# A two-layer hybrid trunk on one core: one weight block kept in dead tables, returned rows read last, modulation weights in longer rows, two modulation tiles moved ahead of a wait

## The reference, cut to what matters

```
for layer in range(DEPTH):
    mod = silu(c) @ ada_w[layer] + ada_b[layer]
    sh_m, sc_m, g_m, sh_f, sc_f, g_f = jnp.split(mod, 6, axis=-1)
    h = _modulate(_rmsnorm(x, norm_mix_g[layer]), sh_m, sc_m)
    m = _attn_lru_mixer(h, ...) if layer % 2 == 0 else _s5_mixer(h, ...)
    x = x + g_m[:, None, :] * m
    h = _modulate(_rmsnorm(x, norm_ffn_g[layer]), sh_f, sc_f)
    x = x + g_f[:, None, :] * _hier_moe(h, ...)      # 16 experts, each frame uses 2
return _rmsnorm(x, final_g)
...
he = jax.nn.silu(t @ w1[e]) * (t @ w3[e]);  out = out + gates[:, e:e + 1] * (he @ w2[e])
```

## Time and profile before

| | us |
|---|---|
| median of 3 runs | 868.66 (868.35 to 869.08) |
| the profiled execution | 869.96 |
| its span | 868.2 |
| PE busy | 796.0 (92%) |
| first matmul on expert weights, layer 0 | 194.6 |
| end of the experts of layer 0 | 427 |
| S5 mixer and GLU of layer 1, end of the last GLU matmul | 548 |
| first gather of the experts of layer 1 | 574 |
| last scatter matmul | 855 |

### The profile page before, as it was taken

The page is one execution under the profiler, slowest core; times in us unless marked ns, Lnnn a source line. Parts: engine busy times, 40 slices in busy tenths (PEclk is TensorE's granted clock), DMA queues, the critical chain, the costliest instruction groups (busy, mean ns, idle before and its releaser), DMA issues.

```text
span 868.2 us, 12685 instructions
## 1 busy us (share of the span) xinstructions
PE 796.0 (92%) x5150; PEld 446.4 (51%) x5151; DVE 345.2 (40%) x701; ACT 194.3 (22%) x325; POOL 183.1 (21%) x288
## 2 busy tenths in 40 slices
PE   2799989999999999999879999779999999989694
PEld 0367643576465465565456544334444756536341
DVE  1436996363041141131389895342000313215124
ACT  2402440251131231221441110421001203101112
POOL 2408779217700000000113300050011112101000
PEclk9899989899999999999999999889999999999897
DMA  9999999957999999999981179923788799999991
GB/s 319 346 354 386 352 358 352 330 209 328 422 421 422 421 421 422 422 422 415 396 325 55 44 280 346 373 85 110 303 316 307 276 421 417 420 420 419 419 413 78
DMA packets 72262, 289.65 MB, mean 334 GB/s; under 512 B 9302, under 2 KB 10614, under 8 KB 47384
## 3 DMA queue, kind: packets, MB, share of 16 engines
q1 hardware_dynamic: 66784, 279.98, 82.4%
q0 software_dynamic: 4736, 7.35, 2.5%
q10 hardware_dynamic: 696, 1.68, 0.5%
HBM read 281.64 MB, written 13.63 MB: 340 GB/s over the span
## 4 chain that ended last, share of the span: by engine, by line
PE 76%; DMA 9%; DVE 9%; ACT 2%; issue 2%; SPq 1%; POOL 1%; DVEq 0%; ACTq 0%; POOLq 0%
PE PS L1939 20%; PE PS L1960 13%; PE PS L1968 7%; PE PS L1942 6%; DMA ring<-in_moe_w 6%; PE PS L2315 6%; PE PS L1992 4%; PE PS L1897 4%; PE PS L1659 3%; DMA work<-in_ada_w 2%; PE PS L1689 2%; PE PS L1763 2%; PE PS L1780 2%; SPq L400 1%; PE PS L2300 1%
## 5 line engine op out<-in xcount | busy, mean ns | idle before, releaser
L1960 PE MATMUL PS<-ring,work 128*64 128x512 f32 (+1 forms) x512 | 129.2, 595 | 2.4 <-DMA ring<-in_moe_w 2.4
L1939 PE MATMUL PS<-ring,hT 128*64 128x256 f32 x896 | 109.3, 387 | 9.8 <-DMA ring<-in_moe_w 9.6
L1939 PE MATMUL PS<-ring,yg 128*64 128x256 f32 x896 | 106.3, 379 | 0.0
L1462 DVE TENSOR_TENSOR work<-work,PS 128x512 f32<-128x512 f32 x32 | 22.0, 687 | 204.0 <-PE PS L1939 154.7
L1939 PEld LDWEIGHTS PS<-ring,hT 128*64 128x64 f32 x896 | 63.0, 138 | 51.2 <-DMA ring<-in_moe_w 12.6
L1960 PEld LDWEIGHTS PS<-ring,work 128*64 128x64 f32 (+1 forms) x512 | 42.9, 143 | 75.5 <-issue 69.5
L1939 PEld LDWEIGHTS PS<-ring,yg 128*64 128x64 f32 x896 | 65.0, 137 | 32.1 <-issue 0.4
L1968 PE MATMUL PS<-work,xhat 128*128 128x256 f32 (+1 forms) x256 | 65.7, 415 | 4.5 <-issue 4.5
L697 POOL DMA_INDIRECT y_rows<-yg,row_no x24 | 23.3, 973 | 187.0 <-DVE yg L1470 154.4
L1968 PEld LDWEIGHTS PS<-work,xhat 128*128 128x128 f32 x256 | 48.7, 193 | 23.9 <-issue 17.9
L937 ACT ACTIVATE work<-PS 128x512 f32<-128x512 f32 x32 | 19.1, 597 | 181.2 <-PE PS L1939 119.9
(11 more groups left out here) (415 smaller groups left out, 1043.8 us busy)
## 6 DMA issues: line engine op xcount, KB each, us to landing
ring<-in_moe_w SPq DMA_DIRECT2D x96, 2048.0 KB, 15.8
ring<-in_ada_w SPq DMA_DIRECT2D x20, 2048.0 KB, 16.2
work<-in_ada_w SPq DMA_DIRECT2D x4, 2048.0 KB, 14.0
ring<-in_s_glu_w SPq DMA_DIRECT2D x4, 2048.0 KB, 13.8
ring<-in_ab_w_in SPq DMA_DIRECT2D x3, 2048.0 KB, 24.3
ring<-in_ab_w_out SPq DMA_DIRECT2D x2, 2048.0 KB, 13.1
ring<-rot_tables SPq DMA_DIRECT2D x2, 2048.0 KB, 17.9
rot_tables<-grow POOLq DMA_DIRECT2D x8, 256.0 KB, 5.6
```

The costliest lines, as they stand in the source:

```text
L1462: v.tensor_tensor(pairs_out(he[:, e % 2, :]), pairs_out(he[:, e % 2, :]), pairs(bank[e % 2 * 2 + 1 if direct else 1]), ALU.mult).then_inc( ...
L1939: last = mm(dst[64 * u:64 * u + 64, 0:256], hg[k][:, e * P:e * P + 64], w[:, k, 256 * u:256 * u + 256], start=k == 0, stop=k == KD - 1)
L1960: last = mm(dst, left[:, at:at + (64 if narrow else P)], w[:, c4, h * HALF:(h + 1) * HALF], start=c4 == 0, stop=c4 == KF - 1)
```

## The change

1. `ada_cut`: tiles 0 to 3 are cut the other way. Each still has 2 MB, but holds two of the eight input blocks for all four output units, in rows of 8 KB. The later tiles go in pairs: four input blocks for two units, in rows of 4 KB. `ada` issues the same eight matmuls of 512 columns a tile; `fold` works in 1024 columns, four instructions a tile.
2. In layer 1 the block w2 3 of the last group is not sent last through `ring`. SP sends it into `kept`, where G1 and G0 were, before the loop over the groups, behind a wait for the last S5 output (`y5_ps`) and the first gather of the layer (`gathered`). PE's `down(3)` reads it there.
3. The four reads of `y_rows` are sent after the remaining blocks. `back` moves up by 4096 columns. `add_back(0)` stands in front of `y_out(2)`, `add_back(1)` in front of `y_out(3)`.
4. `ada(22, 24)` leaves `ffn(1)` and stands in front of the wait for `x_new` 3 (the last new rows of the mixer), behind a wait for `x_part` 5; `ffn(1)` opens with one filler matmul (`keep_busy(6, 1)`), as `ffn(0)` does.

```diff
-        back = w3(T0, 2, NB, D)
+        KEPT = PER_GROUP - 1
+        kept = w3(T0, KF, D)
+        back = w3(T0 + SLOT, 2, NB, D)
...
+        def ada_cut(u):
+            n = ADA_FIRST if u < ADA_FIRST else 2
+            first = u - u % n
+            return first, u % n * (KD // n), KD // n, n
...
-                c0 = u % A_UNITS * HALF
-                sp_.dma_start(ada_unit(u), ada_v[u // A_UNITS, :, :, c0:c0 + HALF]).then_inc(
+                first, k0, n_k, n_c = ada_cut(u)
+                c0 = first % A_UNITS * HALF
+                sp_.dma_start(ada_unit(u), ada_v[u // A_UNITS, :, k0:k0 + n_k, c0:c0 + n_c * HALF]).then_inc(
...
+                if L == 1:
+                    sp_.wait_ge(S("y5_ps"), KD)
+                    sp_.wait_ge(S("gathered"), KD * NG + 1)
+                    sp_.dma_start(kept.rearrange("p (u c) n -> p u (c n)", u=2),
+                                  moe_src(L, "w2", (NG - 1) * EPG + ORDER[KEPT][1])).then_inc(S("cn_in"), 16)
                 with sp_.Fori(0, NG - 1) as i:
...
+                for j in range(SLOTS, KEPT if L == 1 else PER_GROUP):
+                    free_slot(n0 + (NG - 1) * PER_GROUP + j)
+                    send_expert(L, j, NG - 1)
                 if L == 1:
                     sp_.wait_ge(S("spread_out"), 64 + 32 * EPG * DIRECT)
...
-                for j in range(SLOTS, PER_GROUP):
-                    free_slot(n0 + (NG - 1) * PER_GROUP + j)
-                    send_expert(L, j, NG - 1)
...
                     y_out(0)
+                    gated(2)
+                    y_out(1)
+                    gated(3)
                     if L == 1:
                         add_back(0)
-                    gated(2)
-                    y_out(1)
+                    y_out(2)
                     if L == 1:
                         add_back(1)
-                    gated(3)
-                    y_out(2)
                     y_out(3)
...
-                if L == 0:
-                    keep_busy(6, 1)
-                else:
-                    ada(ADA_LAST, ADA_ALL)
+                keep_busy(6, 1)
...
+                        if L == 1 and j == KEPT:
+                            pe.wait_ge(S("cn_in"), 64 + 16)
+                            w2 = kept
...
+            pe.wait_ge(S("x_part"), 5)
+            ada(ADA_LAST, ADA_ALL)
             pe.wait_ge(S("x_new"), 3)
             aside1 = ffn(1)
```

More of the change, by code:

```diff
@@ L332, in unit_dst @@
             return ring[:, n % SLOTS, :]
+        def ada_cut(u):
+            n = ADA_FIRST if u < ADA_FIRST else 2
+            first = u - u % n
+            return first, u % n * (KD // n), KD // n, n
         def ada_unit(u):
-            if ADA_SLOT[u] == "a":
-                return aslot
-            return u3(ADA_SLOT[u])
+            whole = aslot.rearrange("p k c -> p (k c)") if ADA_SLOT[u] == "a" else ring[:, ADA_SLOT[u], :]
+            return whole.rearrange("p (k c) -> p k c", k=ada_cut(u)[2])
         ada_turn = lambda u: 16 * (ADA_SLOT[:u].count(ADA_SLOT[u]) + 1)
@@ L1627, in fold @@
             def fold(u):
-                w, k_of = ada_unit(u), lambda k: condc[:, k:k + 1]
+                first, k0, n_k, n_c = ada_cut(u)
+                m = first - ADA_FOLD
+                total = prods[:, m:m + n_c, :].rearrange("p m n -> p (m n)")
+                w, k_of = ada_unit(u), lambda k: condc[:, k0 + k:k0 + k + 1]
                 dve.wait_ge(S(f"ada_slot_{ADA_SLOT[u]}"), ada_turn(u))
-                link(v.tensor_scalar(w[:, 0, :], w[:, 0, :], k_of(0), None, ALU.mult))
-                for k in range(1, KD - 1):
+                if k0 == 0:
+                    link(v.tensor_scalar(w[:, 0, :], w[:, 0, :], k_of(0), None, ALU.mult))
+                else:
+                    dve.wait_ge(S("ada_used"), u)
+                    link(v.scalar_tensor_tensor(w[:, 0, :], w[:, 0, :], k_of(0), total, ALU.mult, ALU.add))
+                for k in range(1, n_k - 1):
                     link(v.scalar_tensor_tensor(w[:, 0, :], w[:, k, :], k_of(k), w[:, 0, :], ALU.mult, ALU.add))
-                v.scalar_tensor_tensor(folded[u - ADA_FOLD], w[:, KD - 1, :], k_of(KD - 1), w[:, 0, :], ALU.mult,
+                v.scalar_tensor_tensor(total, w[:, n_k - 1, :], k_of(n_k - 1), w[:, 0, :], ALU.mult,
                                        ALU.add).then_inc(S("ada_used"), 1)
@@ L1684, in ada @@
                         pe.wait_ge(S("tab_evac"), 11)
-                    r = u % ADA_EARLY
+                    row, k0, n_k, n_c = ada_cut(u)
                     first, final = [u == b[0] for b in BATCHES], [u == b[1] - 1 for b in BATCHES]
-                    for k in range(KD):
-                        j = k % 4
-                        last = mm(bank[7][32 * j:32 * j + 32, :], condz[:, k, 32 - r:64 - r], ada_unit(u)[:, k, :],
-                                  start=any(first) and k < 4, stop=any(final) and k >= 4)
+                    for n_ in range(n_k * n_c):
+                        j, k, c = n_ % 4, n_ // n_c, n_ % n_c
+                        r = row % ADA_EARLY + c
+                        last = mm(bank[7][32 * j:32 * j + 32, :], condz[:, k0 + k, 32 - r:64 - r],
+                                  ada_unit(u)[:, k, c * HALF:(c + 1) * HALF],
+                                  start=any(first) and n_ < 4, stop=any(final) and n_ >= 4)
                     last.then_inc(S("ada_used"), 1)
```

8 lines of the change are left out of this document (5 added, 3 removed).

## The result

The changed kernel took 863.21 us (median of 9 runs, 860.26 to 866.24) beside 869.08 us of the kernel before (9 runs, 864.6 to 871.93). The ratio is 0.9946, 95% interval 0.9928 to 0.9963, that is -4.7 us (-6.3 to -3.2). The forecast was -9.0 us and a median of 859.7: the sign is right, the time lies inside the range, the gain is about half of what was said. The profiled execution took 865.59 us, its span is 863.8.

What follows compares the result with a forecast made beforehand. PE was taken to bind layer 1's first expert group, the weight stream 690 to 847 us. Terms -1.8 - 3.3 - 3.9 = -9.0 us gave 861.0 profiled, median 859.7; range for 8 in 10, 856.6 to 863.8.

Steps and rivals of the forecast that it cites:

- What bounds the kernel: Layer 1: PE binds the first expert group, the weight stream binds 690 to 847 us; earlier savings move the stream.
- Part 1: Start: longer rows for the modulation tiles bring PE's first projection from 36.2 to 34.4, -1.8 us.
- The rate step: Start, 16 to 30 us: four tiles take 19.9 us at 422 GB/s instead of 21.7 at 387.
- its rival: Start: 8 KB tile rows starve `x`, first projection at 45.5, total 870.8; chance 0.03 without reaching slower, 0.02 slower.
- d: Start: how late `x` lands, put at 13.7 us; slower than before from 11.6.
- 31.8 + d: Start: formula for when the first projection begins if `x` is late by d; it gave 45.5.
- Part 2: Layer 1, after the GLU: two modulation tiles run ahead of the wait for the new rows, -3.3 us.
- the rival of the clock: Layer 1, after the GLU: the clock drops before the turns, -1.5 instead of -3.3 us, total 861.5; chance 0.12.
- Part 3: Tail: one block leaves the stream, returned rows are read last; last scatter ends at 851.2 instead of 855.1, -3.9 us.
- The upper bound: Tail: if PE alone decided, the two scatters would end at 850.1 against 855.1, -5.0 us.
- the rows come late: Tail: returned rows land 2 to 5 us later than computed, total 862 to 865; chance 0.08.
- more at the start: Start: longer rows also take 1.2 us off the first tile, -3.0 instead of -1.8, total 858.5; chance 0.11.

Runs made afterwards that it cites:

- experiment 3: Follow-ups on tail and first gather; among them the changed kernel with five filler matmuls instead of one before layer 1's first gather: 0.9924 of the kernel before.
- rows4k: The changed kernel with modulation tiles 0 to 3 in rows of 4 KB instead of 8 KB: 0.9902 of the kernel before, -8.5 us.
- x_first: The changed kernel with `x` loaded by SP ahead of modulation tile 0 instead of by ACT: 0.9913 of the kernel before, -7.5 us.
- the copies first: The changed kernel with DVE's copies of experts 2 and 3 each put ahead of four additions in the last group: 0.9916 of the kernel before, -7.3 us.
- all repairs and 2 KB rows: The changed kernel with `x` first on SP, copies ahead of additions, longer filler, and modulation tiles in 2 KB rows: 0.9899 of the kernel before, -8.8 us.

## Why the prediction was wrong, point by point

**What bounds the kernel: right.** What the first gather saves is kept to the last gather, microsecond for microsecond (experiment 3), and the end is again the stream and what stands behind it (690 to 842 us at 413 GB/s).

**Part 1, -1.8 us: the step that failed.** The rate step held: 402 to 412 GB/s for 387, and 1.8 us earlier where nothing else is in the way. The failed sentence is "PE's start of the first projection moves from 36.2 to 34.4". It let only the tiles move and held `x` and the small loads of ACT's queue fixed. They share the engines with the tiles, row for row, and `x` came 3.7 us later. The prediction had this mechanism, as its rival, with a chance of 0.05, a price from d = 2.6 on ("eats part 1"), and the sign beyond 11.6; d was 3.7. But by its own formula (31.8 + d) the first projection would have started at 35.5, still 0.7 us earlier than before. The rest of the loss is what it had nowhere: PE's wait of 2.69 us for the small rows behind `x`, and the clock that fell with it (1.7 us).

The rival's d of 13.7 was mis-sized. It took all 2.15 MB that SP had moved by 12.06 as moved beside `x`; of 2.10 MB in the trace 1.15 had passed before the first row of `x` at 5.65, and 0.69 passed beside it. (Two slips: 23 us from the issue at 1.67 end at 24.7, not 25.7, and the wait for the third tile was 0.59, not 0.5.) The prediction set the rival aside on one row, POOL's writes (6.6 against 5.6 us). Those were 256 KB pieces beside 8 KB rows at another time of the program; the 1 MB of `x` in the first microseconds went from 10.4 to 14.0. It also left out the small rows: they were waited for nowhere before, so no row showed them, but they stood behind `x` in its queue. Together +2.1 on the mean where -1.8 was said: 3.9 of the missing 4.3 us.

On the rule of the Trainium skill ("DMA: Bandwidth & Descriptors", section Specifications): it puts full rate at 512 bytes and more. The trace disagrees: 387 GB/s from 16 to 30 us in each of the seven traces with 2 KB rows, 401 to 412 in those with 8 KB rows. The records of the rows agree: one of 2 KB takes 88.7 ns on the mean (before, 16 to 30 us), one of 4 KB 164 (`rows4k`, 16 to 26) and one of 8 KB 315 (`x_first`, 16 to 26), so four of 2 KB take 355.

**Part 2, -3.3 us: right.** -2.9 alone, -3.1 in the distance from the GLU to the last turn; the tiles took 3.64 us (3.84 said), the filler 1.13, the turns ended 9.1 us after the GLU (9 said). In the changed kernel's trace the granted clock stayed at 1.00 from 550 to 558, so the rival of the clock did not come. It did come, at half its price, in two of the twelve traces with part 2: with the copies first the clock was 0.63 and 0.51 from 552 to 556, and the turns ended 10.0 us after the GLU; with all repairs and 2 KB rows it was the same. In the changed kernel's trace the clock fell later: the gather took 17.04 us, 1.4 more than in that of before. But 16.85 was seen without part 2 (the kept block alone), and the mean of the gather is 15.9 us in the nine traces with part 2 and one filler and 15.8 in the five without, so this is the single execution's and not part 2's.

**Part 3, -3.9 us: right, step by step.** From the last gather to the last accumulation 69.5 became 65.5, -4.0; alone it measured -4.3. In times of before (this trace's last gather is 1.3 us earlier) the rows landed at 842.7 (843.0 said), and the last scatter ended at 851.1 (851.2 said). The upper bound, PE alone at 850.1, was reached with the copies first (849.6 in times of before).

**The sum.** +2.1 - 2.9 - 4.0 = -4.8 us, against -4.7 and -4.6 measured. The agreement is better than its parts: the 2.1 is a mean of starts from 36.4 to 39.6, and with the +0.5 that part 1 measured alone the sum would be -6.4. By its number (862 to 865) "the rows come late" came nearest, but the rows came when they were due; "more at the start" did not happen either. Of the signs named beforehand, "`x` lands after 15" was the one that came true.

## What to carry to other kernels

Before making a queue's rows longer, list every transfer on other queues in the same stretch and who waits for each and for what stands behind it in its queue; the ones that are early by a little are the price. Count the rows and not the bytes: each row that is needed waits for one of the other queue's. Put the small and needed transfer first in the same queue as the large ones, rather than beside them. A change of two halves, such as taking a block out of a stream and moving the rows behind it, may be worth its whole gain only together; test the halves before giving one of them away.

## What the runs showed of the hardware

- Two queues with work took turns by rows. Beside rows of 2, 4 and 8 KB, 131, 101 and 67 rows of 4 KB passed on ACT's queue from 6 to 8 us, and 140, 106 and 70 on SP's. A transfer of 1 MB took 10.4, 11.1 and 14.0 us there; with small rows in front of it, 17.8; first in SP's queue, 5.0.
- Rows of 2 KB on full engines moved 387 GB/s in seven traces out of seven; rows of 8 KB 401 to 412 in the same stretch and 422 later. One row took 88.7 ns and 315 ns.
- After PE had stood 3.7 to 5.0 us, 32 matmuls of 512 columns took 15.4 to 17.0 us in 14 traces, and 13.97 in the three in which it had stood under 2 us. A filler of 4.5 us made the difference, and the gather started no later for it.
- The same instructions of the first mixer took 145.2 to 151.7 us from trace to trace. With such scatter a single profile can't size a change of 2 us ahead of them.
